# Feed-forward quarters of two token tiles ahead of the last tile's layer norm

## The reference

```
mix = concatenate([y_pool, y_attn]) @ w_out
h = layer_norm(ALPHA * h + mix, ln1_g, ln1_b)
ff = square(relu(h @ w_ff1)) @ w_ff2          # 1024 -> 4096 -> 1024
h = layer_norm(ALPHA * h + ff, ln2_g, ln2_b)
gate = sigmoid(h @ w_ple_gate + b_ple_gate)
h = h + gate * (p @ w_ple)
```

## Time and profile before

| | |
|---|---|
| median of 3 runs | 1499.66 us (1498.92 to 1499.67) |
| the profiled execution's own time | 1497.15 us |
| its span | 1495.4 us |
| PE busy | 1402.1 us, 94% of the span |
| PE weight loads | 1067.2 us, 71% |
| DVE busy | 957.5 us, 64% |
| ACT busy | 772.8 us, 52% |
| POOL busy | 200.6 us, 13% |
| mean granted clock of PE | 0.969 |

### The profile page before, as it was taken

The page is one execution under the profiler, slowest core; times in us unless marked ns, Lnnn a source line. Parts: engine busy times, 40 slices in busy tenths (PEclk is TensorE's granted clock), DMA queues, the critical chain, the costliest instruction groups (busy, mean ns, idle before and its releaser), DMA issues.

```text
span 1495.4 us, 19865 instructions
## 1 busy us (share of the span) xinstructions
PE 1402.1 (94%) x6629; PEld 1067.2 (71%) x6630; DVE 957.5 (64%) x1154; ACT 772.8 (52%) x963; POOL 200.6 (13%) x235
## 2 busy tenths in 40 slices
PE   7899999999799999999999994979989999999998
PEld 6787667455577777777677763746768888888886
DVE  6845443254899999999998977385644422443185
ACT  4333434123689999999888873344133311342031
POOL 1021001000222122222211220042100000000010
PEclk8999999999999999999999995999989999999999
DMA  6131114306699999999999974122122332233131
GB/s 227 57 113 57 57 42 168 148 17 222 237 400 409 407 417 407 415 411 401 412 403 413 409 243 182 43 70 85 62 92 72 113 113 69 101 113 145 67 113 57
DMA packets 67894, 298.58 MB, mean 200 GB/s; under 512 B 18110, under 2 KB 20220, under 8 KB 55548
## 3 DMA queue, kind: packets, MB, share of 16 engines
q1 hardware_dynamic: 55612, 275.86, 47.7%
q10 hardware_dynamic: 6864, 13.54, 2.5%
q0 software_dynamic: 5360, 8.40, 1.7%
HBM read 292.00 MB, written 14.94 MB: 205 GB/s over the span
## 4 chain that ended last, share of the span: by engine, by line
PE 72%; DVE 6%; DMA 5%; issue 2%; ACT 2%; POOL 1%; DVEq 0%; POOLq 0%; SPq 0%; ACTq 0%
PE ps L714 13%; PE ps L899 12%; PE ps L914 12%; PE ps L752 7%; DMA ring<-in_w_gate 4%; PE ps L745 4%; PE ps L570 4%; PE ps L785 3%; PE ps L723 3%; PE ps L948 3%; PE ps L500 2%; PE ps L451 2%; PE ps L878 1%; PE ps L703 1%; PE ps L604 1%
## 5 line engine op out<-in xcount | busy, mean ns | idle before, releaser
L1997 DVE TENSOR_TENSOR ring_r<-ring,hi 128x2048 fp32r<-128x2048 f32 (+1 forms) x224 | 431.3, 1982 | 17.9 <-ACT hi L1444 15.8
L1444 ACT ACTIVATE hi<-ring 128x2048 fp32r<-128x2048 f32 (+1 forms) x224 | 363.0, 1662 | 11.4 <-DMA ring<-in_w_gate 7.3
L2034 DVE TENSOR_TENSOR ring_r<-ring,ring_two 128x2048 fp32r<-128x2048 f32 (+1 forms) x46 | 102.2, 2260 | 120.7 <-ACT ring_two L1518 120.5
L1518 ACT ACTIVATE ring_two<-ring 128x2048 fp32r<-128x2048 f32 (+1 forms) x46 | 83.9, 1867 | 142.5 <-PE ps L914 121.6
L1117 POOL TENSOR_TENSOR rsv<-msv,half 128x1 f32<-128x1 f32 (+2 forms) x32 | 39.0, 1221 | 722.3 <-DVE msv L1628 702.3
L714 PE MATMUL ps<-ring_r,XTS 128*128 128x512 f32 x512 | 128.6, 394 | 4.8 <-issue 2.5
L914 PE MATMUL ps<-ring_two,ats 128*128 128x512 f32 x512 | 126.6, 389 | 0.0
L714 PE MATMUL ps<-hi,XTS 128*128 128x512 f32 x512 | 126.5, 389 | 0.0
L500 PE MATMUL ps<-ring_r,ring_r 128*128 128x512 f32 x448 | 117.8, 413 | 7.6 <-DVE M L1693 4.5
L752 PE MATMUL ps<-hi,HIDS 128*64 128x512 f32 x512 | 122.9, 392 | 0.0
L714 PEld LDWEIGHTS ps<-ring_r,XTS 128*128 128x128 f32 x512 | 96.9, 190 | 28.2 <-issue 5.8
(11 more groups left out here) (322 smaller groups left out, 2145.2 us busy)
## 6 DMA issues: line engine op xcount, KB each, us to landing
ring<-in_w_up SPq DMA_DIRECT2D x32, 2048.0 KB, 17.1
ring<-in_w_gate SPq DMA_DIRECT2D x32, 2048.0 KB, 14.8
ring<-in_w_down SPq DMA_DIRECT2D x32, 2048.0 KB, 15.8
ring<-in_w_ff SPq DMA_DIRECT2D x16, 2048.0 KB, 8.2
ring<-in_w_in SPq DMA_DIRECT2D x8, 2048.0 KB, 8.0
ring<-in_w_out SPq DMA_DIRECT2D x2, 2048.0 KB
ring<-in_w_ple_gate SPq DMA_DIRECT2D x2, 2048.0 KB
X<-in_x ACTq DMA_DIRECT2D x4, 512.0 KB, 5.0
```

The costliest lines, as they stand in the source:

```text
L1444: act.activation(HI[u][:, c], ring[:, s, c], ACT.Copy).then_inc(w_hi, 1)
L1518: act.activation(hi_of(u, a, part_size(u)), ring[:, s, a:a + part_size(u)], ACT.Copy).then_inc(w2_hi, 1)
L1997: vec.tensor_tensor(ring_r[s][:, c], ring[:, s, c], HI[u][:, c].bitcast(F32), ALU.subtract).then_inc(w_lo, 1)
L2034: vec.tensor_tensor(ring_r[s][:, a:a + n], ring[:, s, a:a + n], hi_of(u, a, n).bitcast(F32), ALU.subtract).then_inc(w2_lo, 1)
```

## The change

- On PE, behind the transposes of tile 2 and ahead of those of tile 3, the first two quarters (f = 0, 1) of `up0` are computed for the tokens of tiles 0 and 1: 2 x 24 matmuls with 256 instead of 512 columns (`up_first`). In `up0`'s own place these two quarters are computed for the tokens of tiles 2 and 3 alone, again 48 matmuls with 256 columns, and only then is the quarter given to ACT. For this, the waits for up0's split and for the low parts of tiles 0 and 1 stand ahead of the new group.
- The transposes of the first norm use the banks 6 and 7, 0 and 1, 6 and 7, 2 and 3 for tiles 0, 1, 2, 3, so that 0 and 1 are free for the two quarters.
- On DVE, the statistics of a half are taken right behind its residual (`half_stats`): those of c = 0 during the products of c = 1 in the first norm, and between the two residuals in the second. `bn` has a row for each tile and half.
- In both norms `h1_rest(t - 1)` or `h5_rest(t - 1)` stands between `ln_stats(t)` and `ln_apply(t)` instead of behind them.

```diff
-        bn = sb("bn", [P, 2, 6])
+        bn = sb("bn", [P, 2 * TT, 6])
...
-                    transposes(("h1", t, c), (0, 1, 6, 7)[(2 * t + c) % 4], X[:, t, c * 512:(c + 1) * 512], 4)
+                    transposes(("h1", t, c), (6, 0, 6, 2)[t] + c, X[:, t, c * 512:(c + 1) * 512], 4)
+
+            def up_first(f, lo, hi, last):
+
+                for i, (a, b) in enumerate(PASSES):
+                    for k in range(DT):
+                        ins = pe.matmul(ps[:, f, lo:hi], weight("up0", a, k * 512 + f * P, P), HTS[b][:, k, lo:hi],
+                                        start=(i == 0 and k == 0), stop=(i == 2 and k == DT - 1))
+                if last:
+                    fill_turn(ins, ("up", f))
...
+            pe.wait_ge(w2_hi, 2 * SPLIT_2.index("up0") + 2)
+            pe.wait_ge(w2_lo, 2 * SPLIT_2.index("up0") + 2)
+            for t in range(TT // 2):
+                left(pe, ("h1", t, 0))
+                left(pe, ("h1", t, 1))
+            for f in range(2):
+                open_turn(pe, ("up", f), f)
+                up_first(f, 0, T // 2, False)
             turn_ln1(TT - 1)
-            for t in range(TT):
+            for t in range(TT // 2, TT):
                 left(pe, ("h1", t, 0))
                 left(pe, ("h1", t, 1))
...
                     for f in range(4):
                         key = ("up", 4 * n + f)
+                        if n == 0 and f < 2:
+                            up_first(f, T // 2, T, True)
+                            continue
...
-            def ln_stats(name, t, key):
+            def half_stats(t, c, key):
+                left(vec, ("o2", c, t) if key == "o2" else ("dn", 1, t, c))
+                step(vec.bn_stats(bn[:, 2 * t + c, :], X[:, t, c * 512:(c + 1) * 512]))
+
+            def ln_stats(name, t):
 
                 b = 48 + 2 * t
-                for c in range(2):
-                    left(vec, ("o2", c, t) if key == "o2" else ("dn", 1, t, c))
-                for c in range(2):
-                    step(vec.bn_stats(bn[:, c, :], X[:, t, c * 512:(c + 1) * 512]))
-                step(vec.bn_aggr(st[:, b:b + 2], bn[:, :, :].rearrange("p a b -> p (a b)")))
+                step(vec.bn_aggr(st[:, b:b + 2], bn[:, 2 * t:2 * t + 2, :].rearrange("p a b -> p (a b)")))
...
             for t in range(TT):
                 residual(0, t, ("o2", 0, t))
+                half_stats(t, 0, "o2")
             ff_unit_lo(0)
...
                 residual(1, t, ("o2", 1, t))
-                ln_stats("l1", t, "o2")
-                ln_apply("l1", t, LNG1, LNB1)
+                half_stats(t, 1, "o2")
+                ln_stats("l1", t)
                 if t:
                     h1_rest(t - 1)
+                ln_apply("l1", t, LNG1, LNB1)
...
                     residual(c, t, ("dn", 1, t, c), 1.0)
-                ln_stats("l2", t, "dn")
-                ln_apply("l2", t, LNG2, LNB2)
+                    half_stats(t, c, "dn")
+                ln_stats("l2", t)
                 if t:
                     h5_rest(t - 1)
+                ln_apply("l2", t, LNG2, LNB2)
```

## The result

| | before | changed |
|---|---|---|
| median | 1498.92 us (1496.45 to 1499.67, 5 runs) | 1489.47 us (1485.16 to 1494.61, 5 runs) |
| ratio | | 0.994, 95% interval 0.9925 to 0.9954 |
| profiled execution, span | 1497.15, 1495.4 us | 1494.61, 1492.9 us |

The account below looks back on a forecast made before the run. PE bounds the kernel, idling 5.3 us in one piece for the first norm's last tile, with its clock halved behind. Terms: -8.5 + 0.3 = -8.2 us, from 1499.66 to 1491.5 us, range 1489.5 to 1496.0.

Parts of the forecast that it names:

- Term 1: First norm, DVE: left half's statistics move under c=1's products; tile 0's transposes and PE's sequence behind them 0.73 us sooner.
- Term 2: First norm, DVE: previous tile's low parts fill POOL's wait (0.51 us a tile); tile 3's norm ready at 1087.15, before 1088.12.
- Term 3: PE's hole before tile 3's transposes: 48 short matmuls at 0.120 us each fill it, from 1081.95 to 1087.71.
- Term 4: From tile 3's transposes to up0's f=2: second halves start 2.9 us later; f=2 gains 8.5 us, 2.03 of it clock.
- Term 5: Second norm: DVE's new order makes PE wait 0.3 us before the last tile's transposes; bounds 0 and 2 us.
- Rival B: Early quarters: a half-width matmul costs about a whole one; loss from a 0.209 us pitch, 1501.7 us at 0.2267; 5%.
- Rival C: Behind tile 3's transposes: PE's clock falls in the remaining 1.9 us gap, second halves pay 2.03 us again; 1493.5 us; 11%.
- Rival D: Both norms: moved low parts make DVE late, with 0.1 us to spare at tile 2; gain 5.5, 1494.2 us; 12%.
- Rival E: Feed-forward behind up0: time saved is given back because up1's weights come late; 1499.7 us; 2%.

Follow-up runs that it names:

- changed_again: The changed kernel, same program, run again; median 1489.86 us, ratio 0.9941 against before; first `mix0` matmul to up0's f=2 63.43 us.
- changed_third: The changed kernel, same program, a third profile, one run; first `mix0` matmul to up0's f=2 61.95 us.
- changed_fourth: The changed kernel, same program, a fourth profile, one run; first `mix0` matmul to up0's f=2 61.98 us.
- lows_behind: The changed kernel with the low parts of tile t-1 behind the norm of tile t again, in both norms; ratio 0.9947 against before.
- one_quarter_lows: The changed kernel with only f=0 early and the first norm's low parts back behind the norm; one run, first `mix0` matmul to f=2 64.50 us.
- pitch: The changed kernel with up1's quarters cut by tokens into matmuls of 512, 256, 384 and 128 columns; 256 columns 0.120 us apart, 384 0.174, 128 0.112.
- dve_only: The kernel before with only DVE's edits (statistics and low parts moved), PE's order old; ratio 0.9991 against before.
- thrown_away: The changed kernel with the early quarters unused: f=0 and f=1 computed anew for all 512 tokens in up0's place; ratio 0.9971 against before.

## Why the prediction was right

The forecast was a gain of 8.2 us, to 1491.5 us, in a range from 1489.5 to 1496.0. Measured are 8.24 us by the two distances, 9.0 (6.9 to 11.2) by the ratio, and a median of 1489.47, which is the lower end of that range to within 0.03 us. That this median lies 2 us under the forecast is not a step of the sum: before's own median moved by 0.74, from 1499.66 to 1498.92, and the other 1.3 us are scatter, since the medians differ by 9.45 here and by 7.8, 8.3 and 8.2 in the later runs of the same two programs (changed_again, and one execution each of changed_third and changed_fourth). The agreement of 8.24 with 8.2 has luck in it as well: in the profile of changed_again the same two distances give 6.8, because the clock fell there.

By its steps, times counted from the first matmul with `mix0` (1034.59 in the profile that it was made from):

- Term 1, tile 0's transposes 0.73 us sooner, the rest of PE's sequence with them: tile 2's were due at 46.57 and came at 46.56. PE's small gap went from 1.30 to 0.57 us. Right.
- Term 2, tile 3's norm ready at 52.56: 52.33. The size was about right (a gain of 0.97 foreseen, 1.20 measured), but the prediction booked it as one gain of two edits. lows_behind and one_quarter_lows separate them: the statistics alone bring the norm forward by 1.92, from 53.53 to 51.61, and the moved low parts take 0.7 us back.
- Term 3, the pitch that no row of before showed: 0.120 taken, 0.120 measured, start at 47.36 against 47.35. The fixed 0.0134 us is right from 256 to 512 columns (pitch), and the waits ahead of the first short matmul were hidden.
- Term 4, f=2 at 61.78: 61.93, a gain of 8.36 for 8.5. PE starts again 2.91 us behind tile 3's transposes (2.9 taken). Only the share that it gave to the clock, 2.03, was too small: that is what up0's first quarters lost, but the transposes and the wait behind them took 3.79 us before (1088.18 to 1091.97) for these 2.91. The sum holds the 0.88 us all the same, since it goes by start times. dve_only against thrown_away gives 3.27 for both parts together, tile 3 to f=2.
- Term 5, a wait of 0.3 us in the second norm: the weight load waits 0.23, its matmul not at all. The prediction set the norm against the time of the load, which runs ahead of the need. R is 0.12 longer, not 0.3; this 0.18 cancels the 0.14 that term 4 lacks, which is luck.
- Rival B (a pitch of 0.21 or more) is out. The estimate of 0.216 us from the Trainium skill (TensorE: Matmul & The Clock Gate) put load and matmul one behind the other; they overlap here, at 0.120 us. Its other half, a load of 107 ns for 128 columns (section "LDWEIGHTS (loading the stationary operand)"), fits the 0.112 at 128 columns.
- Rival C (the clock falls in the last gap all the same) got 11%. It isn't one case or the other: it came in one of four profiles of the changed kernel, and cost 1.50 us there, not 2.03. How many of the unprofiled executions it came in isn't known; their median may hold some of it.
- Rival D: the 0.1 us to spare at tile 2 was enough; PE had no wait there. Rival E: the distance behind f=2 is the same in every kernel of the table.

## What to carry to other kernels

When an engine waits for the last part of its input, look for later work that needs only the parts already there, and cut it to them so that it fits into the wait. Here that was half the tokens: two matmuls of 256 columns cost 0.0134 us more than one of 512, and no more. Cut to 128 columns a matmul would still have taken 0.112 us, hardly less than the 0.120 of 256. Price a hole of TensorE with the clock behind it: 2.5 of 8.4 us came back by merely keeping the engine busy. And when two edits touch one chain, ask for each alone: the low parts that were moved into POOL's wait of 0.5 us take 1.3 there, and only the cover of another edit made them free.

## What the runs showed of the hardware

- The granted clock behind a gap of PE of 1.88 us, with 0.9 us of transposes right ahead of it and full work before, is not a property of the program: the same one kept 1.00 in three profiles and had 0.68 over 5.4 us in one. Gaps of 4.80 (dve_only) and 5.25 us (before) were followed by 0.50.
- fp32r matmuls with a 128 x 128 stationary operand start 0.227, 0.174, 0.120 and 0.112 us apart for 512, 384, 256 and 128 columns (before and pitch, granted clock 1.00).
- In the second norm PE's weight load stands 0.23 us ahead of its matmul (1446.61 and 1446.84); when the load of the last tile waited 0.23 us, the matmul still came 6.32 us behind the one before it, as in the kernel before.
